# Attention of the second mixer with four buffers of softmax weights, and reciprocals and gate products taken for two units at once

## What is computed

```
p_cmp = masked_softmax(einsum('bsghd,bcgd->bghsc', q, k_cmp) * scale, cmp_mask)
...
p = masked_softmax(einsum('bqghd,bgqkd->bghqk', qb, kg) * scale, mask)      # selected blocks
...
p = masked_softmax(einsum('bqghd,bkgd->bghqk', qb, kb) * scale, mask)       # window
...
o = gate[..., 0:1] * heads(o_cmp) + gate[..., 1:2] * heads(o_sel) + gate[..., 2:3] * heads(o_win)
return (o.reshape(B, S, NSA_INNER) * jax.nn.silu(z)) @ w_out
```

## Time and profile before

| | us |
|---|---|
| median of 3 runs | 1899.04 (1898.32 to 1901.15) |
| the profiled execution, its own time | 1899.72 |
| its span in the profile | 1898.0 |
| TensorE busy over the span | 1824.1 (96%) |
| VectorE, ScalarE, GpSimd busy | 1095.2, 675.3, 308.9 |

### The profile page before, as it was taken

One profiled execution on the slowest core, in us unless ns is written; L12 is line 12 of the kernel. 1 busy time (PEld: TensorE's weight loads), 2 busy tenths in 40 slices (PEclk: granted clock), 3 DMA queues, 4 the chain that ended last, 5 costly groups with the idle time before them and its releaser, 6 DMA issues. The chain is left out here.

```text
span 1898.0 us, 36850 instructions
## 1 busy us (share of the span) xinstructions
PE 1824.1 (96%) x15870; PEld 1484.7 (78%) x15870; DVE 1095.2 (58%) x1644; ACT 675.3 (36%) x1100; POOL 308.9 (16%) x292
## 2 busy tenths in 40 slices
PE   8999999999999788999999899999999999999997
PEld 6877757688888567778888669888878888888886
DVE  4664354553257788444366887778574635354545
ACT  4334332332223577442222374433233322122342
POOL 4210011130002565320021240000001000000011
PEclk9999999999999899999999999999999999999998
DMA  5334323142223010134421100002042322322221
GB/s 191 103 111 134 136 83 133 45 190 101 90 74 111 35 37 12 49 109 138 137 102 56 48 2 4 4 3 70 4 178 92 104 104 89 111 89 89 78 100 45
DMA packets 42848, 160.87 MB, mean 85 GB/s; under 512 B 5312, under 2 KB 14528, under 8 KB 28096
## 3 DMA queue, kind: packets, MB, share of 16 engines
q1 hardware_dynamic: 28480, 143.84, 22.1%
q10 hardware_dynamic: 14208, 14.68, 2.2%
HBM read 140.42 MB, written 16.78 MB: 83 GB/s over the span
## 5 line engine op out<-in xcount | busy, mean ns | idle before, releaser
L257 DVE TENSOR_TENSOR wlo<-raw,whi 128x2048 fp32r<-128x2048 f32 (+2 forms) x113 | 251.0, 2221 | 179.2 <-ACT whi L248 178.8
L248 ACT ACTIVATE whi<-raw 128x2048 fp32r<-128x2048 f32 (+2 forms) x113 | 209.0, 1850 | 320.8 <-PE ps L283 161.4
L281 PE MATMUL ps<-act_hi,whi 128*128 128x512 f32 x616 | 243.1, 395 | 0.0
L301 PE MATMUL ps<-act_lo,whi 128*128 128x512 f32 x632 | 242.7, 393 | 0.0
L283 PE MATMUL ps<-act_hi,wlo 128*128 128x512 f32 x616 | 240.6, 391 | 0.0
L282 PE MATMUL ps<-act_lo,whi 128*128 128x512 f32 x616 | 240.5, 390 | 0.0
L300 PE MATMUL ps<-act_hi,whi 128*128 128x512 f32 x592 | 236.4, 399 | 0.0
L305 PE MATMUL ps<-act_hi,wlo 128*128 128x512 f32 x632 | 156.5, 389 | 0.0
L301 PEld LDWEIGHTS ps<-act_lo,whi 128*128 128x128 f32 x632 | 120.2, 190 | 25.9 <-issue 1.2
L305 PEld LDWEIGHTS ps<-act_hi,wlo 128*128 128x128 f32 x632 | 118.6, 188 | 24.7
L300 PEld LDWEIGHTS ps<-act_hi,whi 128*128 128x128 f32 x592 | 111.6, 188 | 32.5 <-issue 8.2
(11 more groups left out here) (550 smaller groups left out, 3474.7 us busy)
## 6 DMA issues: line engine op xcount, KB each, us to landing
raw<-stream_in SPq DMA_DIRECT2D x107, 1024.0 KB, 4.9
v_scratch<-v_out ACTq DMA_DIRECT2D x16, 256.0 KB, 3.5
z_scratch<-zt ACTq DMA_DIRECT2D x16, 256.0 KB, 2.9
mlh_v<-v_scratch SPq DMA_DIRECT2D x4, 1024.0 KB, 4.8
mlh_z<-z_scratch SPq DMA_DIRECT2D x16, 256.0 KB, 2.6
cmp_w<-cmp_w_in SPq DMA_DIRECT2D x2, 2048.0 KB, 11.3
z_scratch<-in_zt ACTq DMA_DIRECT2D x16, 256.0 KB, 3.2
mix_g<-z_scratch SPq DMA_DIRECT2D x16, 256.0 KB, 6.6
```

Source lines behind the costliest of these rows:

```text
L248: act.activation(k.whi[b % 2][:, 0:n], k.raw[b % RAW_SLOTS][:, 0:n], ACT.Copy).then_inc(k.hi_done, 1)
L257: dve.tensor_tensor(k.wlo[b % 2][:, 0:n], k.raw[b % RAW_SLOTS][:, 0:n], k.whi[b % 2][:, 0:n].bitcast(F32), ALU.subtract).then_inc(k.lo_don ...
L281: pe.matmul(bank, hi, x_hi, start=(x == 0), stop=False)
L301: pe.matmul(bank, hi, x_lo, start=False, stop=False)
```

## The change

The weights get a fourth buffer (`DEEP = 4`), and everything behind the exponentials moves by a step: TensorE transposes unit n-3 in step n, and takes the values of a pair in odd steps; the copies are those of unit n-3. Reciprocal and gate product are made once for both units of a pair (`pair`, 4 columns instead of 2), in even steps n, for units n-2 and n-1, and the two multiplications by the factor follow one another. The `att_y` product moves from n % 4 = 3 to n % 4 = 0. The name `COPIES` replaces a constant and has the same value: ScalarE still copies both halves for 512 keys, and the added `if` is never true. The fourth buffer takes the place of `nsa_q_hi1`, which moves into a slot for raw weights that is free in the attention, and with it the split of query tiles 2 and 3 moves from ScalarE and VectorE in the stage before to GpSimd at the start of the attention.

```diff
-    k.q_hi = [k.region(f"nsa_q_hi{i}", [P, 2, S], F32R, at) for i, at in enumerate((62.5, 28))]
+    k.q_hi = [k.region("nsa_q_hi0", [P, 2, S], F32R, 62.5), k.at("nsa_q_hi1", [P, 2, S], F32R, 60 + 8 * (b1 % RAW_SLOTS))]
...
-    high_at = (17, 18, 23, 23, 24, 24, 25, 25)
+    high_at = (17, 18, 23, 23, None, 24, None, 25)
...
-    p = k.region("att_p", [P, 3, 2, S], F32, 16)
+    DEEP, COPIES = 4, TT - 1
+    p = k.region("att_p", [P, DEEP, 2, S], F32, 16)
...
+    def pair(base, c):
+        return k.small[:, base + 4 * (c % 2):base + 4 * (c % 2) + 4]
...
+            for t in (2, 3):
+                high(t)
+                low(t)
             for m in range(U):
                 L = length(m)
-                pool.wait_ge(s["w_done"], m + 1)
+                pool.wait_ge(s["w_done"], m // 2 + 1)
...
-            for n in range(U + 3):
+            for n in range(U + DEEP):
                 if n + 1 < U:
                     scores(n + 1)
-                if 2 <= n < U + 2:
-                    m = n - 2
+                if DEEP - 1 <= n < U + DEEP - 1:
+                    m = n - DEEP + 1
...
-                if n >= 4 and n % 2 == 0:
-                    c = n // 2 - 2
+                if n > DEEP and n % 2:
+                    c = (n - DEEP) // 2
...
-                        if n >= 3:
-                            act.wait_ge(s["tr_mm"], n - 2)
-                        act.activation(p[:, n % 3, e, 0:L], k.ps[:, 2 * (n % 2) + e, 0:L], ACT.Exp,
+                        if n >= DEEP:
+                            act.wait_ge(s["tr_mm"], n - DEEP + 1)
+                        act.activation(p[:, n % DEEP, e, 0:L], k.ps[:, 2 * (n % 2) + e, 0:L], ACT.Exp,
...
-                if n >= 7 and n % 4 == 3:
-                    u = (n - 7) // 4
+                if n >= 8 and n % 4 == 0:
+                    u = (n - 8) // 4
...
-                if 1 <= n <= U:
-                    m = n - 1
-                    t, i, br = units[m]
-                    dve.wait_ge(s["exp_done"], 2 * m + 2)
-                    steps.then_wait(dve, dve.reciprocal(sm(24, m), sm(8, m)))
...
+                if 2 <= n <= U and n % 2 == 0:
+                    c = n // 2 - 1
+                    t, i, br = units[n - 2]
+                    dve.wait_ge(s["exp_done"], 2 * n)
+                    steps.then_wait(dve, dve.reciprocal(pair(24, c), pair(8, c)))
...
+                    for m in (n - 2, n - 1):
+                        L = length(m)
+                        dve.tensor_scalar(p[:, m % DEEP, 1, 0:L], p[:, m % DEEP, 1, 0:L], sm(32, m)[:, 1:2], None, ALU.mult) \
+                            .then_inc(s["scaled1"], 1)
```

More of the change, by code:

```diff
@@ L1687, in score_low @@
                 whole, hi, lo = parts(n)
-                dve.wait_ge(s["score_hi"], n + 1)
+                dve.wait_ge(s["score_hi"], 1 + sum(at is not None for at in high_at[:n]))
                 dve.tensor_tensor(lo, whole, hi.bitcast(F32), ALU.subtract)
@@ L1766, in _ @@
                 for n in range(8):
-                    if high_at[n] == t - 1:
+                    if high_at[n] is not None and high_at[n] == t - 1:
                         score_low(n)
@@ L1803, in sm @@
         return k.small[:, base + 2 * (n % 4):base + 2 * (n % 4) + 2]
+    def pair(base, c):
+        return k.small[:, base + 4 * (c % 2):base + 4 * (c % 2) + 4]
     def copied(eng, m):
         eng.wait_ge(s["pt1"], m + 1)
-        own = sum(i < TT - 1 for _, i, _ in units[:m + 1])
+        own = sum(i < COPIES for _, i, _ in units[:m + 1])
         if own:
@@ L1891, in _ @@
                                 rows, at = rows_half(half), (TT * e + j) * P // 2
-                                last = pe.transpose(k.ps[:, 4 + half, at:at + P // 2], p[rows, m % 3, e, j * P:(j + 1) * P],
+                                last = pe.transpose(k.ps[:, 4 + half, at:at + P // 2], p[rows, m % DEEP, e, j * P:(j + 1) * P],
                                                     k.const("ident")[rows, rows])
                     last.then_inc(s["tr_mm"], 1)
-                if n >= 4 and n % 2 == 0:
-                    c = n // 2 - 2
+                if n > DEEP and n % 2:
+                    c = (n - DEEP) // 2
                     u = c // 2
@@ L1925, in high @@
                     act.activation(k.act_hi[:, 4 * gp + 2 * e + x, :], y[:, x, e, :], ACT.Copy).then_inc(s["y_hi"], 1)
-            for n in range(U + 2):
+            for n in range(U + DEEP - 1):
                 if n < U:
@@ L1949, in _ @@
                     else:
+                        if units[m][1] >= COPIES:
+                            out, src = turned(m, 0)
+                            act.activation(out, src, ACT.Copy)
                         out, src = turned(m, 1)
@@ L1968, in low @@
                     dve.tensor_tensor(k.act_lo[:, tile, :], y[:, x, e, :], k.act_hi[:, tile, :].bitcast(F32), ALU.subtract)                         .then_inc(s["y_lo"], 1)
-            for n in range(U + 4):
+            for n in range(U + DEEP + 1):
                 if n < U:
@@ L1990, in _ @@
                                       z[:, x, :, at], ALU.mult).then_inc(s["y_done"], 1)
[L1991 to L2006 removed]
+                if 2 <= n <= U and n % 2 == 0:
[3 more added lines that the diff above has]
+                    steps.then_wait(dve, dve.reciprocal(pair(24, c), pair(8, c)))
+                    if c >= 2:
+                        dve.wait_ge(s["scaled0"], n - 4)
+                        dve.wait_ge(s["scaled1"], n - 4)
+                    gates = k.gtok[:, i, :].rearrange("p (a e h b) -> p a h b e", a=2, e=2, b=3)
+                    dve.tensor_tensor(pair(32, c).rearrange("p (h e) -> p h e", e=2), pair(24, c).rearrange("p (h e) -> p h e", e=2),
+                                      gates[:, t // 4, t % 4:t % 4 + 2, 1 + br, :], ALU.mult).then_inc(s["w_done"], 1)
+                    dve.wait_ge(s["w_done"], c + 1)
+                    for m in (n - 2, n - 1):
+                        L = length(m)
+                        dve.tensor_scalar(p[:, m % DEEP, 1, 0:L], p[:, m % DEEP, 1, 0:L], sm(32, m)[:, 1:2], None, ALU.mult) \
+                            .then_inc(s["scaled1"], 1)
+                if DEEP - 1 <= n < U + DEEP - 1 and units[n - DEEP + 1][1] < COPIES:
+                    m = n - DEEP + 1
                     L = length(m)
```

27 lines of the change are left out of this document (7 added, 20 removed).

## The result

The changed kernel took 1905.46 us (median of 15 runs, 1901.12 to 1910.14). The kernel before, beside it on the same chip, took 1899.59 (15 runs, 1896.67 to 1903.1). The ratio, which is estimated from the single runs and isn't the quotient of the medians, is 1.0027, 95% interval 1.0019 to 1.0035: slower, and above the range of the prediction. The profiled execution took 1903.63 us with a span of 1901.9, against 1899.72 and 1898.0. I followed ScalarE's rows through both traces: up to the stage before the attention they are 0.2 us apart. TensorE leaves the attention 3.3 us later (778.89 against 775.56), and at the end the rows are 3.9 us later. So most of what there is to explain lies in this stage.

A forecast was written before the change was run, and what follows sets the result against it. No engine was taken as full: TensorE busy 125.1 of the attention's 149.5 us, VectorE 118.7. The stage before (1.6) plus the attention (0.6) gave 2.2 us less, 1896.8; range 1892, less the median's spread, to 1901.7.

The forecast's parts named there:

- two multiplications: VectorE's work ahead of maximum 17 in the attention's second group: two multiplications taken as 0.42 us, beside maximum, att_y and copy.
- The layout by hand: Attention's second group of 16 units timed in the new order: scores(32) at 34.95 us after scores(16) instead of 35.45.
- k_lo: VectorE subtraction in the stage before the attention: escapes GpSimd's product, 0.68 us instead of 1.77; next z tile 1.70 earlier.
- Scores(22): TensorE in the attention's second group: these scores start 12.86 us after scores(16), instead of 15.0.
- The maximum of the odd unit becomes the bound: Rival, attention: one multiplication more ahead of that maximum costs up to 9.8 us, 1906.6; half, 1901.7, at most placeable; chance 0.12.
- at few keys scores run ahead: Argument against the odd-maximum rival: scores run ahead of TensorE's other work, so only half the 9.8 us can be placed.
- The waits at transposes go: Rival, attention: TensorE's 12.4 us of idle time ahead of transposes vanish, 1886 us; with half of them, 1892; chance 0.34.
- The stage before: Stage ahead of the attention: two subtractions leave VectorE, the last z tile and the attention's start come 1.6 us earlier.
- move along: From the last z tile to the attention's start: 4.36 us of silu, store and semaphores stay as long, only shifted earlier.
- GpSimd's four operations: Two casts and two subtractions at the attention's start: under 7.5 us, cost nothing; without cover up to 2 us once.
- reciprocals and gates x32: Sign to look for in the attention's profile: reciprocals and gate products counted x32; 8 of each removed in a group.
- the end of 7 to 8 us: Sign at the attention's end: 7 to 8 us from the last scores to the next stage's first matmul; 7.0 before.

The follow-up runs named there:

- the short multiplication: The changed kernel with VectorE multiplying the odd unit's product by the constant 1.0 instead of its weights: 1902.62 us, ratio 1.0005 to the kernel before.
- the copy set first: The changed kernel with VectorE's copy of unit n-3 right behind the maximum, ahead of the paired work: 1938.82 us, ratio 1.0212 to the kernel before.

## Why the prediction was wrong

**The step that failed: "two multiplications" at 0.40 each.** The layout by hand took the multiplication's start-to-start distance from the earlier trace rows, where each stands alone on VectorE and a copy or a maximum out of PSUM follows. In the pair the second one starts while GpSimd's first product is underway. Measured: 1.24 us instead of 0.80 at 512 keys, and by the means 0.32, 0.22 and 0.11 us more at 384, 256 and 128; eight pairs of each size make 8.6 us of VectorE's time (8 x (0.42 + 0.32 + 0.22 + 0.11)). Pairing removed 32 x 0.39 = 12.5 us of reciprocals and gate products. What was left of that brought no measurable time: with the 12.5 us gone and the multiplications apart the ratio is 0.9994, with the split alone 0.9987. And the lengthened row lies ahead of a maximum that ScalarE waits for. The two kernels with the same instructions in the same order, of which one has that row short, have ratios of 1.0030 or 1.0027 and 1.0005: about 4.5 us of the loss, out of 5 to 6.

The prediction had a warning. It had worked out from the earlier trace rows that a VectorE operation on two SBUF tiles is held up by GpSimd's, and used it for k_lo in the stage before. The multiplication reads one tile and a column, and alone it starts just ahead of GpSimd's (670.09 and 670.15 in the earlier trace rows) and takes 0.49 us; but whether a second one behind it, with GpSimd underway, would be held up too, the prediction did not ask.

**The rest of the layout.** With the second multiplication short, as the layout had it, the second group still takes 35.73 us and not 34.95. Scores(22) come at 13.04, 0.18 late, so up to there the method was good; 0.6 us are lost behind; by the releasers these are waits of transposes for GpSimd and the copies, which I had put too low. The stage as a whole was forecast 0.6 us shorter, came 4.3 longer, and is 1.6 longer with the short multiplication. So some 2.2 us of the miss in the profile are these waits, 2.7 the lengthening; the medians give the lengthening more, 4.5, with some 2.5 us of uncertainty, which the intervals of the two ratios leave. A part of it may be low clock behind the attention, as the last section shows.

**The rival.** "The maximum of the odd unit becomes the bound" is what happened, at 0.12. Its full price was 9.8 us, over the time of the forecast, and named 1906.6; 1905.5 was measured. But its reckoning, one multiplication more of ordinary length, isn't what the runs show: with that alone the ratio is 1.0005. Its argument that at few keys scores run ahead, and so half at most, holds for the ordinary length only.

**"The waits at transposes go"** failed as argued: they stayed (14.4 us), with the copies as releaser. But "releaser" did not mean cause there: the copy set first made the kernel 2.1% slower.

**The stage before.** The rule drawn from the earlier trace rows was right for k_lo, 0.68 us. The last z tile came 1.49 us earlier, near the 1.6 of the forecast, although the rotation's swapped rows now make VectorE wait 0.92 us. What failed is the step behind it, that the 4.36 us of silu, store and semaphores "move along": they became 4.90, and 4.62 in the run with the split alone, so that 0.95 us arrived. Why they grew no run tells. The split on GpSimd cost nothing, as said: that part alone has 0.9987.

**GpSimd's four operations, reciprocals and gates x32, the end of 7 to 8 us** came as forecast (7.4).

The balance: the moved split gives some 2.5 us (0.8 to 4.2). The fourth buffer and the joint reciprocals, measured together with it, add nothing (0.9994 with both, 1.0000 with the buffer alone), and the two multiplications side by side take back 5 or more. No version that I ran is measurably faster than the kernel before by more than 0.2%. The best is the moved split alone, 0.9987; its time is below that of both kernels.

**What stays open.** Why a second multiplication by a column of weights is caught beside GpSimd and one by a constant is not, in the same place and at the same distance, no run tells. I can also not say how the remaining ratio (1.0005 with the short second, 0.9994 with it behind the next maximum) divides, since the intervals touch.

## What to carry to other kernels

When two like operations are put side by side on one engine, and the same semaphore lets another engine go on the same memory, don't price the second by a row in which it stood alone: look for a row of the profile where the two engines overlap, and take that. Fewer instructions on an engine that isn't full brought nothing measurable here, since they did not bring forward what someone waits for; put the shared work behind that and not ahead of it. And a releaser in a row is the last to come, which need not be the one to move: moving it made the kernel 2.1% slower here.

## What the runs showed that I had not expected

**VectorE beside GpSimd, both in SBUF, 128x512.** The first multiplication took 0.49 us throughout; the second, by a column of weights, 0.92 right behind it (0.84 from start to start) and 0.75 with a copy out of PSUM between; 0.49 with GpSimd held; by a constant 0.42. GpSimd's mean was 1739 ns in the first case, 1641 held, 1845 with the constant. In the kernel before, where each of its products starts with one multiplication of VectorE's, it was 1873 (1.86 in the earlier trace rows); so there it is GpSimd that pays some 0.2 us. So neither waited out the other's whole instruction, as the reading of the earlier trace rows had it for k_lo: the second was 0.43 us longer, beside a product of 1.7. The Trainium skill (SBUF — State Buffer, "Who interferes with whom") has the whole instruction as the unit of such a wait, for a tensor_scalar that runs in a mode with both ports as well (no row shows the mode); for this pair of operations the measurement differs, and it decides.

**The spread of the changed kernel's times does not come from this stage, and much of it goes with TensorE's clock.** The two profiled executions of the changed kernel have stages of 153.7 and 154.0 us, but times of 1903.63 and 1908.55. Right behind the attention the longer one, shown first, has the granted clock at 0.72 and 0.60 of full speed, so at the level of 1.2 GHz for most of 780 to 785 us, where the other has 1.00:

```profile
775.00:780.00 5.00, 3.88 (x35) 3.04 (x36) 1.50 (x5) 1.19 (x4) 1.03 (x2) 0.72 0.01 3
780.00:785.00 5.00, 5.00 (x16) 3.89 (x14) 3.66 (x4) 2.32 (x2) 0.00 (x0) 0.60 0.00 0
```

```profile
775.00:780.00 5.00, 3.33 (x37) 2.67 (x38) 1.98 (x8) 1.23 (x5) 1.27 (x2) 1.00 0.01 3
780.00:785.00 5.00, 5.00 (x24) 4.14 (x23) 3.92 (x5) 2.42 (x3) 0.00 (x0) 1.00 0.00 0
```

In 780 to 785 us TensorE starts 16 matmuls in the one and 24 in the other. In both, TensorE had been busy for only 3.3 to 3.9 of the 5 us before. ScalarE's rows put 2.4 us of the difference in this place. Another 2.6 arise between 1180 and 1400 us, where the granted clock of the longer one is 0.91 (1320 to 1340) and 0.74 (1380 to 1400) against 1.00 and 0.84; that all of this part is clock is not shown. A single profiled execution can thus lie 5 us off another of the same kernel, as much as this change costs.

This bears on the loss too. Of the 27 times of the changed kernel, 10 lie by themselves between 1907.9 and 1910.2 us; no time of the kernel before is above 1905.8, and with the short multiplication one of 11 is above 1906, at 1907.3. Without these 10 the medians of the two series are still 3.7 and 4.5 us above the kernel before. So the stage's loss stands, and the upper bunch adds 0.9 to 1.7 us to it. The one profile that I have of it, 1908.55, is the one with the low clock right behind the attention; what brings that clock about is open.
